# Down projection of a Fourier-mixing feed-forward block: one level of Strassen's method on 512-wide chunks

## What is computed

```python
mod_x = silu(c) @ w_ada + b_ada                 # shift, scale, gate, twice
sh1, sc1, ga1, sh2, sc2, ga2 = split(mod_x, 6)
hx = rmsnorm(x, g_mix) * (1 + sc1) + sh1
x = x + ga1 * (real_fft(hx) @ fno_w_out)        # 512 tokens, 2048 channels, 4 groups
h2 = rmsnorm(x, g_ffn) * (1 + sc2) + sh2
x = x + ga2 * (square(relu(h2 @ w_ffn_in)) @ w_ffn_out)   # 2048 -> 8192 -> 2048
return rmsnorm(x, g_final)
```

## Time and profile before

| | us |
|---|---|
| median of 3 runs | 1756.23 (1755.89 to 1758.16) |
| span of the profiled execution (page) | 1753.6 |
| the same, from first to last instruction of the core (views of the trace) | 1751.8 |
| TensorE busy | 1708.3 (97%) |
| VectorE busy | 797.3 (45%) |
| ScalarE busy | 453.6 (26%) |
| GpSimd busy | 25.8 (1%) |

### The profile page before, as it was taken

The page is one execution under the profiler, slowest core; times in us unless marked ns, Lnnn a source line. Parts: engine busy times, 40 slices in busy tenths (PEclk is TensorE's granted clock), DMA queues, the critical chain, the costliest instruction groups (busy, mean ns, idle before and its releaser), DMA issues.

```text
span 1753.6 us, 18033 instructions
## 1 busy us (share of the span) xinstructions
PE 1708.3 (97%) x7797; PEld 1393.9 (79%) x7797; DVE 797.3 (45%) x500; ACT 453.6 (26%) x412; POOL 25.8 (1%) x16
## 2 busy tenths in 40 slices
PE   4999999999999999999999999999999999999997
PEld 3767788777888888888888888888888888888886
DVE  5657897575443344334433443344334433443344
ACT  5441222442211221122122112211221122112214
POOL 0000000000000000000000000000000000000013
PEclk9999999999999999999999999999999999999999
DMA  8888999667333223322332233233223322332212
GB/s 353 315 331 337 374 351 366 218 238 278 109 96 96 96 97 96 96 96 96 96 96 96 96 96 96 96 98 97 92 97 104 98 92 100 104 98 93 99 48 96
DMA packets 93154, 264.11 MB, mean 151 GB/s; under 512 B 4112, under 2 KB 5440, under 8 KB 79680
## 3 DMA queue, kind: packets, MB, share of 16 engines
q1 hardware_dynamic: 92768, 262.50, 42.9%
q0 software_dynamic: 208, 1.07, 0.2%
q10 hardware_dynamic: 144, 0.07, 0.0%
HBM read 259.42 MB, written 4.19 MB: 150 GB/s over the span
## 4 chain that ended last, share of the span: by engine, by line
PE 94%; DMA 2%; DVE 2%; ACT 1%; issue 1%; SPq 0%; POOLq 0%; POOL 0%; DVEq 0%; ACTq 0%
PE banks L935 31%; PE banks L936 30%; PE banks L937 30%; PE banks L953 1%; DMA raw<-in_w_ffn_in 1%; DVE acc_a L639 1%; DMA xres<-in_x 1%; DMA raw<-in_w_ada 0%; PE banks L998 0%; ACT wsp L436 0%; PE banks L1039 0%; PE banks L969 0%; DVE xres L815 0%; DVE gated L809 0%; ACT xsp L415 0%
## 5 line engine op out<-in xcount | busy, mean ns | idle before, releaser
L732 DVE TENSOR_TENSOR wsp<-raw,wsp 128x2048 fp32r<-128x2048 f32 x144 | 331.6, 2303 | 715.4 <-ACT wsp L436 715.3
L436 ACT ACTIVATE wsp<-raw 128x2048 fp32r<-128x2048 f32 x144 | 276.0, 1916 | 972.3 <-PE banks L937 854.9
L935 PE MATMUL banks<-acts,wsp 128*128 128x512 f32 x1024 | 400.3, 391 | 2.4 <-DVE acts L863 2.4
L935 PE MATMUL banks<-wsp,hid 128*128 128x512 f32 x1024 | 398.5, 389 | 2.0 <-ACT gate L558 2.0
L937 PE MATMUL banks<-acts,wsp 128*128 128x512 f32 x1024 | 399.1, 390 | 0.0
L936 PE MATMUL banks<-acts,wsp 128*128 128x512 f32 x1024 | 398.9, 390 | 0.0
L936 PE MATMUL banks<-wsp,hid 128*128 128x512 f32 x1024 | 398.4, 389 | 0.0
L937 PE MATMUL banks<-wsp,hid 128*128 128x512 f32 x1024 | 398.3, 389 | 0.0
L935 PEld LDWEIGHTS banks<-acts,wsp 128*128 128x128 f32 x1024 | 192.7, 188 | 42.7 <-DVE acts L863 3.1
L935 PEld LDWEIGHTS banks<-wsp,hid 128*128 128x128 f32 x1024 | 192.3, 188 | 42.6 <-ACT gate L558 2.8
L937 PEld LDWEIGHTS banks<-acts,wsp 128*128 128x128 f32 x1024 | 192.5, 188 | 40.1
(11 more groups left out here) (130 smaller groups left out, 837.0 us busy)
## 6 DMA issues: line engine op xcount, KB each, us to landing
raw<-in_w_ada SPq DMA_DIRECT2D x96, 1024.0 KB, 7.1
raw<-in_w_ffn_in SPq DMA_DIRECT2D x64, 1024.0 KB, 5.3
raw<-in_w_ffn_out SPq DMA_DIRECT2D x64, 1024.0 KB, 5.0
raw<-in_w_mix SPq DMA_DIRECT2D x16, 1024.0 KB, 7.1
xres<-in_x SPq DMA_DIRECT2D x4, 1024.0 KB, 8.1
out<-xres SPq DMA_DIRECT2D x4, 1024.0 KB, 4.1
raw<-in_seq_table SPq DMA_DIRECT2D x1, 1024.0 KB, 13.5
gfin<-in_g_final POOLq DMA_DIRECT2D x1, 1024.0 KB, 4.9
```

The source lines that it names most:

```text
L436: nc.scalar.activation(wsp[:, ws, 0, :, :], raw[:, slot, :].rearrange("p (a n) -> p a n", a=UK), ACT.Copy).then_inc(w_hi, 1)
L732: nc.vector.tensor_tensor(wsp[:, ws, 1, :, :], raw[:, slot, :].rearrange("p (a n) -> p a n", a=UK), wsp[:, ws, 0, :, :].bitcast(F32), ALU. ...
L935: nc.tensor.matmul(bank, w_hi_ap, m_hi, start=first, stop=False)
```

## The change

The up and the down projection now work on 16 chunks of 512 hidden channels (`CH`). The down projection of one chunk is done by one level of Strassen's method, in Winograd's form: the hidden activations (512 tokens x 512 channels) are cut into quarters of 256x256, and the weights into two pairs of blocks of 256x512 for each of two column halves (`PAIRS`). In place of 8 quarter products there are 7 (`PRODUCTS`), some of them on sums and differences of quarters.

- Weights are split in steps of half a unit (128x1024) into four slots (`stp`, same memory as `wsp`). A period has 22 steps: for each column half the order is u 0 1 u 2 u 3 u 4 5 6, where u is 24 matmuls of the next chunk's up projection and a digit is one of the seven products of this chunk's down projection, 12 matmuls. There are 15 periods. In front stand the 8 up steps of chunk 0 (the prelude) and behind them the 14 products of chunk 15 alone (the last stretch).
- Weight sums: four subtractions of 128x1024 in each column half, on VectorE, in place in the raw slots (`half_sum`). Hidden sums: four of 128x512 per chunk on VectorE (`hidden_low`).
- Each product leaves PSUM by itself: VectorE adds its two banks to an accumulator in SBUF (`sum_read`, 128x1024). Products 0, 2, 4, 6 use banks 4 and 5, and 1, 3, 5 use banks 6 and 7. Products 2, 3 and 6 go on accumulating onto what the bank holds, and the bank is read again.
- The accumulators `dacc` take the place of `xres`. The mixed x is written to DRAM after the mixing stage by four 1 MB transfers from GpSimd's queue, and read back at the end into `xmix`.
- The gate's 16 vector steps are spread: 8 in the prelude, 2 in each half of periods 0 and 1. The gate's sum over partitions moves into the last stretch.
- At the end VectorE forms the remaining sums (`combine`), the gate product and the residual (`finish`, eight blocks of 128x1024), and the normalisation follows in two steps of two token tiles.

The core of the diff:

```diff
-    CH = 1024
+    CH = 512
+    half_steps = ["u", 0, 1, "u", 2, "u", 3, "u", 4, 5, 6]
+    gate_runs = [[("ada", GATE2, k) for k in range(a, b)] for a, b in ((0, 8), (8, 12), (12, 16))]
+    def used_before(i):
+        return (3, 3, 3, 7)[i % HS] if i % HS < 4 else 4
+    quarters = [sq[:, 0:HALF_T, 0:N // 2], hsum[:, :, :], sq[:, HALF_T:HT, 0:N // 2], sq[:, HALF_T:HT, N // 2:N],
+                sq[:, 0:HALF_T, N // 2:N], hsum[:, :, :], hsum[:, :, :]]
+    DEST = (3, 3, 0, 2, 3, 3, 1)
# SP, loads of a period: up, left, right, up for each column half
+    for j, w in enumerate(period_units):
+        if j >= RAW:
+            sp.wait_ge(w_lo, freed_at(p, period_units[j - RAW]))
...
+        load(w, slot_of(p, w), p + 1 if w[0] == "up" else p)
# GpSimd
+    pool.wait_ge(x_updated, DB)
+    for t in range(TT):
+        pool.dma_start(xmix_d[t * P:(t + 1) * P, :], xres[:, t, :]).then_inc(spilled, 16)
# ScalarE, prelude
+    act.wait_ge(w_used, MU - 1 if m < 2 else MU if m in (2, 5) else MU + m - 2)      # up_high(m)
...
+        if k % 2 == 1 and k // 2 + 2 < UPS:
+            up_high(k // 2 + 2)
# ScalarE, a period
+    act.wait_ge(w_used, used + 1)                     # step_high: used = step_at(p, i) - used_before(i)
+    HID_AT = {PS - 2: 0, PS - 1: 1, 0: 2, 1: 3, 2: 4, 3: 5, 4: 6}
+    for i in range(PS):
+        step_high(*next_step(p, i + 3))
+        if i == PS - 4:
+            hidden_relu(p + 1, step_at(p, i + 1))
+        if i in HID_AT:
+            hidden_high(p + 1 if i > HS else p, HID_AT[i])
...
+    hidden_relu(0, U0)                                # before period 0
+    for i in range(3):
+        step_high(0, i)
+        if i >= 1:
+            hidden_high(0, i - 1)
# VectorE, prelude
+        if k % 2 == 1 and k // 2 + 2 < UPS:
+            up_low(k // 2 + 2)
+        if k % 4 == 3:
+            gate2(gate_runs[0][k // 2 - 1:k // 2 + 1])
# VectorE, weight sums
+        if w == 1:
+            nc.vector.tensor_tensor(t1, t1, b11, ALU.subtract).then_inc(t_sum, 1)
+        elif w == 3:
+            nc.vector.tensor_tensor(t1, b22, t1, ALU.subtract).then_inc(t_sum, 1)
+            nc.vector.tensor_tensor(b21, t1, b21, ALU.subtract).then_inc(t_sum, 1)
+        elif w == 4:
+            nc.vector.tensor_tensor(b11, t1, b11, ALU.subtract).then_inc(t_sum, 1)
# VectorE, a period
+    for i in range(PS):
+        step_sum(*next_step(p, i + 4))
+        step_low(*next_step(p, i + 3))
+        sum_read(p, i)
+        if i == PS - 3:
+            hidden_square(p + 1)
+        if i in HID_AT:
+            hidden_low(p + 1 if i > HS else p, HID_AT[i])
+        if isinstance(p, int) and p < UNROLLED and i % HS == HS - 4:
+            gate2(gate_runs[1 + p][2 * j:2 * j + 2])
# VectorE, the last stretch
+    for i in range(len(last_steps)):
+        if i + 4 < len(last_steps): step_sum(PERIODS, i + 4)
+        if i + 3 < len(last_steps):
+            if last_steps[i + 3][1] in LATE_SUMS: half_sum(PERIODS, *last_steps[i + 3])
+            step_low(PERIODS, i + 3)
+        sum_read(PERIODS, i)
...
+        if w == 5: combine(j, 2, 2 * j + 1)
+        if w == 6 and j == 0: combine(0, 1, 2)
+        if j == 1 and w < 4: finish(w)
+    for i in range(4, 7): finish(i)
+    combine(1, 1, 4)
+    finish(7)
# TensorE, one product (12 matmuls)
+    if j == 0:
+        pe.wait_ge(h_lo, PRODUCTS * p + q + 1)
+    pe.wait_ge(d_read, base + (0, -1, 1, 2, 3, 4, 5)[q])     # base: products of earlier halves
+    for tt in range(2):
+        for kk in range(HALF_T):
...          # three matmuls of 512 columns, high*high, high*low, low*high
+    mm.then_inc(w_used, 1)
```

More of the change, by code:

```diff
@@ L91, in fourier_ffn_block, with step_at, prelude_slot, slot_at @@
     table_order = [("seq",), ("cos",), ("sin",)]
[L92 to L102, removed]
+    position = {w: u for u, w in enumerate(units)}
+    def step_at(p, i):
+        return p * PS + (U0 + i)
+    def used_before(i):
+        return (3, 3, 3, 7)[i % HS] if i % HS < 4 else 4
+    def prelude_slot(m):
+        return (m + (2 if m < 2 else 3)) % SLOTS
+    def slot_at(i):
+        return i % HS % SLOTS
     fills = [0] * RAW
@@ L276, in unit_source @@
                 if w[0] == "up":
[L277 to L279 removed]
+                    return up_v[:, UK * w[1]:UK * (w[1] + 1), bass.ds(chunk * CH, CH)]
+                first = w[1] * COLS + (HALF_D if w[0] == "right" else 0)
+                return down_v[:, bass.ds(chunk * HT, HT), first:first + COLS]
             def consumed(w):
@@ L545, in hidden_high @@
[L545 to L577, removed]
-                nc.scalar.activation(xres[:, t, 0:D // 2], gained[:, t, 0:D // 2], ACT.Copy,
-                                     scale=inv[:, 2, t:t + 1]).then_inc(y_scaled, 1)
@@ L582, in _, with hidden_relu @@
-            for t in range(TT):
-                block_squares(2, DB - 1, Y1 + DB * CHUNKS, [t])
-                act.wait_ge(mean_done, 3 + t)
+            def hidden_relu(chunk, used):
+                act.wait_ge(w_used, used)
+                if isinstance(chunk, int) and chunk == 0:
+                    act.wait_ge(h2_lo, DT)
+                else:
+                    act.wait_ge(h_lo, PRODUCTS * chunk)
+                for half in range(2):
+                    nc.scalar.activation(sq[:, HALF_T * half:HALF_T * (half + 1), :],
+                                         banks[:, HALF_T * half:HALF_T * (half + 1), :], ACT.Relu)\
+                        .then_inc(h_relu, 1)
@@ L1169, in _, with up_step @@
-            chunk_body(0)
-            with pe.Fori(1, CHUNKS) as chunk:
-                chunk_body(chunk)
+            def up_step(slot, m, first):
+                for kk in range(2):
+                    k = 2 * m + kk
+                    if first:
+                        if k + LEAD < DT:
+                            turn_tokens(k + LEAD)
+                        pe.wait_ge(h2_lo, k + 1)
+                    for f in range(HT):
+                        cols = slice(P * f, P * (f + 1))
+                        mm = product(banks[:, f, :], stp[:, slot, 0, kk, cols], stp[:, slot, 1, kk, cols],
+                                     acts[:, k, 0, :], acts[:, k, 1, :], k == 0, k == DT - 1)
+                mm.then_inc(w_used, 1)
```

505 lines of the change are left out of this document (354 added, 151 removed).

## The result

The changed kernel takes 1790.08 us (median of 4 runs, 1784.39 to 1795.09), the kernel before 1756.06: a ratio of 1.0195 (95% interval 1.018 to 1.0211), so nearly 2% slower. The forecast was 1786.2. The profiled execution has a span of 1787.1, against 1751.8 before by the same measure: 35.3 us more, where the sum said 30.0. (The median lies 3.0 above this span, not 4.4 as taken in the forecast, so the forecast time is only 3.9 off.)

The account below looks back on a forecast made before the run. TensorE was taken to bound the kernel, 97% busy, if VectorE stays in time. Terms -87.0 + 39.1 + 10.7 - 1 + 18 + 32.5 + 17.7 = +30.0 gave span 1781.8, median 1786.2, 1.7% slower; 8-in-10 range 1757 to 1818.

Parts of the forecast that it names:

- Matmuls: Down projection: 2688 matmuls in place of 3072, 384 fewer at 0.2266 us each, -87.0 us.
- Periods: Three TensorE stops a period (1.08 twice before product 6, 0.48 before product 0): 84.24 for 81.6, +39.1 us in all.
- Prelude: Up steps of chunk 0: stops at tiles 3, 5, 7, 9, 11 (+8.7) and the DRAM write (2): +10.7 us.
- Start of period 0: First up step waits 4.5 us for relu, high and low part, against 5.56 before: -1 us.
- Gate steps in periods 0 and 1: Their loads share raw slots, so up units land late and product 6 comes 4.5 later in four halves: +18 us.
- Last stretch: Chunk 15's products without up steps: VectorE's queue sets the time, 70.6 us for 38.1 of matmuls, +32.5.
- End: From last matmul to kernel end: 28.4 us against 10.7, +17.7, with GpSimd's gain just keeping up.
- The clock: TensorE's clock may fall in the last stretch, 4.4 us in the range, 0 in the sum; periods unchanged.
- (2): Rival: VectorE never holds TensorE in the periods; periods and gates cost 0, -27 us, 1729, faster; chance 0.15.
- (3): Rival: loads late in every half, 1 to 3 us a half, +30 to 60 more, about 1830; chance 0.10.
- (4): Rival: restarts at each of 22 steps with two or three waits cost 36 us more, 1822; chance 0.07.
- (5): Rival: gain and cost of the whole change cancel, within 0.2%; chance 0.04.

Follow-up runs that it names:

- reads first: Against the changed kernel, VectorE reads each finished product before the next weight sum and low part in every step of a period; 1746.1 us, 0.9942 of the kernel before.

## Why the prediction was right, step by step

- **Matmuls, -87.0.** 384 fewer, 0.2266 apart. The steady period of 81.60 with reads first is 360 x 0.2266 = 81.6.
- **Periods, +39.1.** Measured 84.21 a period, and its three stops separated by two runs into 2.13 and 0.48. Right to 0.03 us a stop.
- **Prelude, +10.7.** From the first up matmul to the end of the prelude 396.88 - 328.62 = 68.3 against 57.97, with the start 0.3 later: +10.6. The size was right by luck, by errors that cancel. The stops are shorter than forecast (3.27, 0.88, 0.60, 1.42, 3.27 idle; 3.5, 2.5, 0.9, 2.5, 3.6 forecast), and the 2 for the write are nothing; in their place stand 3.0 us that TensorE lost to its lower clock, see below.
- **Start of period 0, -1.** 401.28 - 396.88 = 4.4 against 5.56.
- **Gate steps in periods 0 and 1, +18.** The first three periods are 15.4 longer than a start without clock loss and without them would be. 13 go with the gate steps, and some 1.9 is low clock after the start: without gate steps the relu of period 1 still comes 477.62 - 401.01 = 76.6 after the first step, where the forecast's clock gives 74.7. The mechanism, reads that come late behind loads, was right; as stops it was worth 7.7 and not 18, and the clock made up part of the rest.
- **Last stretch, +32.5.** 72.1 for 38.1 of matmuls: +34.0, bound by VectorE as said:

```profile
1679.92:1752.03 72.11, 51.65 (x177) 37.30 (x176) 63.19 (x57) 22.91 (x35) 12.73 (x5) 0.88 0.11 42
```

VectorE is busy 63.19 of 72.11 (88%, 90% forecast). That it is the bound shows in another way too: from the last relu to the last matmul it is 81.1 to 81.2 us in all seven runs whose code is the same there, whatever TensorE's clock did. Without GpSimd's gain it is 78.1, so 3.0 of the 34.0 are VectorE standing still beside GpSimd, as above, which the sum had at nothing; without them this term is 31.0.
- **End, +17.7.** This step failed. 1787.1 - 1752.03 = 35.1 against 10.7: +24.4. The term said of GpSimd's gain, "each beside VectorE's `finish`", that "it just keeps up". It does, but VectorE doesn't: three operations take 3.25 in place of 1.22, and one of 0.75 takes 2.25. Without the gain the end is 1772.0 - 1744.47 = 27.5, by the forecast's own reckoning 28.4. The trace of the kernel before could have shown it, though no row that the prediction used does. VectorE's low part of 128x2048 (two SBUF inputs) takes 2.29 everywhere else, but twice it began while GpSimd was at work, and took 2.86 and 3.35:

```profile
1707.19 4.61 POOL L338 TENSOR_TENSOR gained<-xres,gfin 128x2048 f32<-128x2048 f32 x1 [6.76 <-DVE xres L793]
```

```profile
1710.61 3.35 DVE L732 TENSOR_TENSOR wsp<-raw,wsp 128x2048 fp32r<-128x2048 f32 x1 [3.50 <-ACT wsp L436]
```

It ends at 1713.96, 2.16 after GpSimd's end at 1711.80. There it cost nothing, as TensorE didn't wait for it. A group's mean hides this; the single records show it.

The sum of what was measured: -87.0 + 39.1 + 10.6 - 1.2 + 15.4 + 34.0 + 24.4 = 35.3, the whole difference of the spans. That the sum came within 5.3 of it is in part luck. In the prelude and behind the gate steps the stops were forecast 28.7 us long in all (8.7, 2 and 18) and were some 15.0 (7.3 more than in the kernel before and 7.7 more than without the gate steps), and TensorE's clock, forecast at 0 there, took 10.2.

**The clock.** The forecast kept it at 0 in the sum, weighed it for the last stretch alone, and said the periods would not change. The steady ones don't. But the same forecast had stops of 3.5 in the prelude and of 4.5 behind the gate steps, and there TensorE's clock did fall. TensorE alone, in the stretches behind the stops of 3.27, 4.23, 4.54 and 1.90 us and in the last stretch (length, busy, granted clock):

```profile
343.00:346.00 3.00, 2.92 (x7) 0.50 0.97 336
346.50:349.00 2.50, 2.50 (x17) 1.00 1.04 406
...
401.20:404.00 2.80, 2.72 (x6) 0.50 0.00 0
...
534.80:538.00 3.20, 3.13 (x8) 0.50 0.97 353
...
581.80:585.10 3.30, 3.30 (x9) 0.50 0.48 174
...
1719.00:1725.00 6.00, 5.98 (x14) 0.50 0.00 0
```

0.50 is the lower of the two levels, matmuls 0.43 apart in place of 0.227. Such a fall costs some 1.4 to 1.6 us on top of the stop, and 2.9 behind the one of 4.54 (14 matmuls x 0.2). Added up over the starts in TensorE's timeline it is 3.0 us in the prelude and 7.2 in the first three periods, against 1.7 there without the gate steps. The length of the stop alone doesn't say whether the clock falls. In the changed kernel it fell behind stops of 1.90, 2.72 and 3.27 and more; it didn't behind those of 0.82, 1.51 and 2.39. With reads first the same stop of 3.27 before tile 11 was followed by full clock:

```profile
382.40:385.40 3.00, 3.00 (x14) 1.00 0.96 341
```

The clock also goes with the differences between executions of one kernel: the four of the changed kernel took 1784.39, 1788.73, 1791.42 and 1795.09, with mean granted clocks of 0.981, 0.978, 0.976 and 0.974. The Trainium skill, TensorE: Matmul & The Clock Gate, HAM oscillation, has this as a reason against gaps in TensorE's work, and here the trace agrees. The runs with fewer stops bear it out at the start of period 0: with the stop at 2.12 instead of 4.23 the first matmuls run at full distance, and the relu of period 1 follows 467.67 - 392.82 = 74.9 after the start. But that run also lacks the stop of 1.08 and still has the gate steps, so it bounds the cost and doesn't measure it.

Of the rivals, (2), no stop in the periods, fell by the profile and was made true for the steady periods by one change of order; (3) and (4), late loads in all halves and restarts, fell with the period of 81.60; (5), that gain and cost cancel, fell with the time.

## What to carry to other kernels

Average load says little: VectorE was busy 72% and held up TensorE in every period, because an operation that had to wait for TensorE stood in its queue ahead of the one that TensorE waited for. Write down, for each wait of the bounding engine, what is queued ahead of its releaser and what that in turn waits for; then put what releases it first, and work whose inputs are not ready yet last. A method that saves matmuls can have a stretch where its extra vector work has no matmuls of other work beside it, here the last chunk and the end, and that part, 58 us of 87 here, decides whether it pays.

## What the runs showed of the hardware that was not expected

- A VectorE operation of 128x1024 with two SBUF inputs that begins while GpSimd works on SBUF ends 1.08 or 1.09 after GpSimd does: 3.25 in all beside a GpSimd operation of 3.26. One of 128x2048 ended 2.16 after it in the kernel before. One that began before, or that reads PSUM and SBUF, takes its 1.21 or 1.22. A scaling (one SBUF input, 0.75) was held as well: 2.25.
- GpSimd's operation of 128x1024 takes 2.34 to 2.40 us when no such VectorE operation is running at its start, and 3.20 to 3.29 when one began just before it. The 0.9 between them is about what the VectorE operation had left (1755.82 + 1.22 - 1755.98 = 1.06), so the wait seems to go both ways.
- Behind stops of 1.90 us and more TensorE often ran at half clock, for 3 to 6 us of its work; the same stop of 3.27 did it in one run and not in another. So a broken-up stretch costs more than its stops, and by an amount that changes from one execution to the next.
